# A hybrid attention block and an AdaLN block on one core: ScalarE's steps of attention and planes one slot later, the query norm in the logits, modulation tiles placed anew

## The chip, the cores and the metric

One of the eight cores of a Trainium2 chip runs the whole kernel. The metric is the device time in microseconds of one execution, here the median of three runs. "Slot", "unit" and "tile" below are the kernel's own terms and are explained where it is described.

## The reference, cut to what matters

Sequence 256, width 2048, batch 1, all in fp32. A first block puts 16 meta tokens ahead of the sequence (272 tokens) and runs one layer of two branches. A second block runs on the result with a modulation vector made from a condition `c`.

```python
# first block
q = apply_partial_rope(rms_norm(q_a.reshape(B, T, H_A, HD_A), q_norm_g), *rope_a)   # 8 heads of 128
k = apply_partial_rope(rms_norm(k_a.reshape(B, T, KV_A, HD_A), k_norm_g), *rope_a)
o_a = dsa_attention(q, k, v, qi, ki, wi, chunk_ids, topk)   # indexer scores, top 64 keys, softmax(q.k * d**-0.5)
o_b = hgrn2_chunkwise(qb, 1.0 - f, vb, jnp.log(f))          # gated linear recurrence
merged = sum over the branches of sigmoid(gate) * (y @ w_branch);  x = x + merged @ w_out
# second block
mod = silu(c) @ ada_w + ada_b; sh1, sc1, g1, sh2, sc2, g2 = split(mod, 6)           # ada_w is 2048 x 12288
h  = modulate(rmsnorm(x, norm1_g), sh1, sc1);  hc = modulate(rmsnorm(ctx, norm1_g), csh1, csc1)
q, k, v, f, hy = split(h @ w_in);  kc, vc = split(hc @ w_in[:, 1024:3072])
a = neighbourhood_attention(q, k, v, kc, vc, rpb)
y = merge_groups(a, fourier_mix(f), hyena_mix(hy, ...), mix_norm_g)
x = x + g1 * (y @ w_out)
x = x + g2 * conv_gated_mlp(modulate(rmsnorm(x, norm2_g), sh2, sc2), ...)
return rmsnorm(x, final_norm_g)
```

## The kernel before, in words

**Number format.** Every fp32 value that goes into a large product is split into a high and a low part ("planes", hi and lo) of the type fp32r, and a product is three: hi·hi, lo·hi and hi·lo (lines L1779 to L1781, L1791 to L1793 and L1801 to L1803 for the three layouts). Activations lie with features on partitions (`phi`, `plo`: 16 planes of 128 x 256).

**Slots.** All large products are cut into 668 chunks of 128 x 1024 or equal-sized weights; a unit is four chunks (two in OA and OB). The phases, with their first slot: FB 0, QB 16, IB 32, QI 48, K 64, KA 68, QA 76, VA 92, ZB 100, ZA 116, GA 132, GB 164 (projections of the first block), E 196 (branch products), F 228 (output product, residual), G 260, H 276, IH 292, IF 316, J 324, IQ 340 (projections of the second block: context and stream), OA 372, OB 388 (output), L 404 (MLP up), M0 580 and M1 624 (MLP down). In slot c TensorE multiplies chunk c, ScalarE makes the high part of the weights of chunk c + 4 (`whi`, L558; it waits for TensorE to be done with chunk c), VectorE the low part (`wlo`, L1087; it waits for the high part). There are four buffers of each.

**Side work.** Each engine's order is written out by hand, slot by slot: after the chunk's own step come the steps attached to that slot. They are the recurrence (slots 16 to 91), norms and rotations of attention's chunks from S_NK = 92, the indexer and top k from S_IX = 121, attention from S_AT = 146 (one head and query half per slot, 16 slots), y at S_Y = 167, the squares of the context from S_CQ = 206, the context's planes from S_CX = 231, the stream's planes from S_X1 = 266, filters, Hyena, the Fourier part and neighbourhood attention in the phases G to OA. An instruction that waits holds up all that follows it in its engine's order.

The steps that matter here:
- first planes: ScalarE copies x to `phi` (L862), VectorE makes `plo` (L1109) and the tmp before it (L1112), in slots 4 to 15 and the next.
- norms of the chunks of attention (nine of 13: four of k, the indexer's key, four of q): squares on ScalarE (L767), a mean over the head by a product with a constant matrix (L1931), root on ScalarE (L781), reciprocal and gain on VectorE (L1393, L1394). The rotation is a product with a permutation (L1925) and three VectorE steps (L1401 to L1403).
- attention, head step a: logits on TensorE (L1963), scale, mask and maximum on VectorE (L1444, L1445), exp on ScalarE (L800), division by the sum on VectorE (L1429, L1430), three transposes on TensorE (L1969 to L1971), their copy on ScalarE (L807, L808), three products with v (L1955 to L1957), copy of the result on VectorE (L1438).
- context in F: VectorE multiplies a plane by gain and inverse root (L1512), ScalarE makes `c_hi` (L889), VectorE `c_lo` (L1508) one slot later.
- stream in G and H: VectorE `ptmp` (L1532), ScalarE `stream_hi` (L909), VectorE `stream_lo` (L1537) one slot later.
- neighbourhood attention: the bias is gathered by 16 small loads (L491), two constants by two more (L492, L493); the flip product (L2107) uses them at S_FLIP = 349. L2117 and L982 belong to the mixing of heads behind it.

**Modulation.** `ada_w` is read in 96 tiles of 1 MB. Tiles 0 to 31 are multiplied on TensorE (L1815), 32 to 95 on VectorE in two halves, each in a slot of its own (`ada_half`, L1147 and L1150). At the end of each section of 16 tiles TensorE sums over partitions (L1844); the slots are in `CLOSE`.

**Loads.** SyncE's queue brings everything. Weights (L390) and tiles (L399) share a ring of four raw buffers of 1 MB: entry e is issued when entry e − 4 has been released, by VectorE's `wlo` for weights, by the tile's use for tiles. The order of entries is the order of the units, a tile behind the weights of its unit; where a tile is used is set by `ada_tile_at`.

Of the kernel before, what the change touches and what calls it, by code (L numbers as in the profile page):

```python
# [77 lines left out]
for _n in ("GB", "E"):  # L78
    for _u in range(0, 8, 2):
        ada_tile_at(U0[_n] + _u, -2, 2048)  # L80
for _u in range(8):
    ada_tile_at(U0["F"] + _u, -2, 20480)
for _u in range(8):
    ada_tile_at(U0["G"] + _u, -2, 24320)
for _u in range(7):
    ada_tile_at(U0["IH"] + _u, -2 if _u else 0, 10240)
# [3 lines left out]
for _u, _off in enumerate((2, 1, 0)):  # L90
    ada_tile_at(U0["IQ"] + _u, _off, 8192)
for _u, _off in enumerate((2, 1, 0, -2, -2)):
    ada_tile_at(U0["IQ"] + 3 + _u, _off, (21504, 20480))
for _u in range(0, 12, 2):
    ada_tile_at(U0["OA"] + _u, -2, (21504, 20480))
for _u in range(1, 32, 2):
    ada_tile_at(U0["L"] + _u, -2, 22528)
HOP_F, HOP_IH, HOP_J, FIRST_J, HOP_IQ, HOP_Y = 40, 56, 63, 64, 66, 69


CLOSE = [(0, 15, SH1, ADA_SLOT[15]), (16, 31, SC1, ADA_SLOT[31]), (32, 47, G1, START["F"] + 30), (48, 63, SH2, START["J"] + 8),
         (64, 79, SC2, START["OB"] + 6), (80, 95, G2, ADA_SLOT[95] + 4)]
# [25 lines left out]
TURN_AT.update({(U0["VA"] + 1 + _n // 2, 2 * (_n % 2)): 8 + _n for _n in range(4)})  # L128
# [12 lines left out]
S_BEXP, S_KD, S_KDT, S_OUT = 64, 68, 74, 84  # L141
S_NK, S_IX, S_TOP, S_IX1, S_TOP1, S_AT, S_Y = 92, 121, 129, 133, 141, 146, 167
# [3 lines left out]
S_CQ, S_CX, S_X1, S_SIN = START["E"] + 10, START["F"] + 3, START["G"] + 6, START["G"] + 2  # L146
# [17 lines left out]
def program(nc, A, out):  # L164
# [5 lines left out]
    with ctx:  # L170
# [99 lines left out]
        L, P, PT = R(13920, 2, T), R(14464, 3, T), R(15280, 2, 384)  # L270
# [75 lines left out]
        NNORM = 9  # L346

        def rope_of(c):
# [9 lines left out]
            gain = {1: cols[:, V_KN:V_KN + 1], 2: cols[:, V_QN:V_QN + 1], 3: cols[:, V_IK:V_IK + 1], 0: None}[kind]  # L358
# [6 lines left out]
        def _(sp):  # L365
# [116 lines left out]
            for i in range(8):  # L482
                if i == 3:
# [49 lines left out]
        def _(act):  # L533
# [57 lines left out]
            def evacuate(u):  # L591
# [8 lines left out]
                elif name in ("IB", "VA"):  # L600
                    k = 2 * i + (8 if name == "VA" else 0)
                    act.wait_ge(S("mm"), C0[u + 1])
                    if k >= 1:
                        act.wait_ge(S("vt_tp"), k)
                    for h in range(2):
                        c = nc.scalar.activation(vT[:, h, :], ps[2 * p + h][:, 0:T], ACT.Copy)
# [9 lines left out]
                elif name == "QA":  # L616
                    ev_T(u, q_a[:, 512 * i:512 * i + 512], 256)
# [151 lines left out]
            def attention(s):  # L769
# [23 lines left out]
                a = s - S_AT  # L793
                if 0 <= a < 16:
                    act.wait_ge(S("at_max"), a + 1)
                    if a >= 3:
                        act.wait_ge(S("at_tp"), a - 2)
                    if a >= 2:
                        act.wait_ge(S("at_norm"), a - 1)
                    nc.scalar.activation(P[:, a % 3, :], L[:, a % 2, :], ACT.Exp, bias=small[:, 8 + a % 2:9 + a % 2],  # L800
                                         accum_out=small[:, 10 + a % 2:11 + a % 2]).then_inc(S("at_exp"), 1)
                b = a - 3
# [51 lines left out]
            for c in slots("FB", "GB"):  # L854
# [5 lines left out]
                for kt in PL_AT.get(c, []):  # L860
                    act.wait_ge(S("pl_tmp"), kt + 1)
                    nc.scalar.activation(phi[:, kt, :], xT[:, kt, :], ACT.Copy).then_inc(S("pl_hi"), 1)  # L862
                if (u, q) in TURN_AT:
                    tokens_of(TURN_AT[u, q])
                if u == U0["K"] + 1 and q == 0:
# [6 lines left out]
            def context(s):  # L872
# [8 lines left out]
                if s == S_CQ + 8:  # L881
                    act.wait_ge(S("x_mean"), 2)
# [129 lines left out]
            for c in slots("E", "OB"):  # L1012
# [15 lines left out]
                if 0 <= c - S_X1 < 16:  # L1028
                    kt = c - S_X1
# [34 lines left out]
        def _(dve):  # L1064
# [39 lines left out]
            def first_planes(s):  # L1104


                for kt in PL_AT.get(s - 1, []):
# [17 lines left out]
            def ada_half(c, n, half):  # L1125


                e = ENTRY["ada", n]
# [4 lines left out]
                elif n == HOP_F:  # L1133
                    dve.wait_ge(S("x_mean"), 2)
# [108 lines left out]
            def slot(c):  # L1243
# [20 lines left out]
                if c in ADA_HALF:  # L1264
                    ada_half(c, *ADA_HALF[c])
# [119 lines left out]
            def attention(s):  # L1385
# [40 lines left out]
                b = s - S_AT - 1  # L1426
                if 0 <= b < 16:
                    dve.wait_ge(S("at_exp"), b + 1)
                    chain(v.reciprocal(small[:, 12:13], small[:, 10 + b % 2:11 + b % 2]))  # L1429
                    v.tensor_scalar(P[:, b % 3, :], P[:, b % 3, :], small[:, 12:13], None, ALU.mult).then_inc(S("at_norm"), 1)  # L1430
                    own("at_norm")
                b = s - S_AT - 4
                if 0 <= b < 16:
                    qt, h = b // 8, b % 8
                    dve.wait_ge(S("at_pv"), b + 1)
                    if b < 12:
                        dve.wait_ge(S("at_qk"), b + 5)
                    v.tensor_copy(o_a[:, 256 * h + 128 * qt:256 * h + 128 * qt + 128], ps[4 + b % 2][:, 272:400]).then_inc(S("att_out"), 1)  # L1438
# [901 lines left out]
```

## Time and profile before

| | us |
|---|---|
| median of 3 runs | 2317.23 (2315.51 to 2318.69) |
| the profiled execution | 2316.17 |
| its span | 2314.4 |
| TensorE busy | 2202.2, mean granted clock 0.986 |
| VectorE busy | 1467.1 |
| ScalarE busy | 1029.1 |
| read from memory | 465 MB, 202 GB/s over the span |

The span is from the first to the last instruction that the profiler recorded; the difference of 1.8 us to the time lies around it. In the rows, PE is TensorE, PEld its weight load, DVE VectorE, ACT ScalarE, SP SyncE. A row of the trace gives the start, the time from start to end, the instruction with its output and inputs, how many of them follow each other (x), and in brackets how long the engine had been idle before it and what ended that. An instruction on TensorE is pipelined: the next one begins before the record of the last ends. The granted clock is a share of TensorE's full 2.4 GHz; the lower level is 1.2 GHz.

### The profile page before, as it was taken

The page shows a single profiled execution, that of the slowest core. Times are in us where ns is not written, and L with a number is a line of the kernel's source. Part 1 is how long each engine was busy: PE and PEld are TensorE (multiplying, and loading weights), DVE is VectorE, ACT ScalarE, POOL GpSimd, SP SyncE. Part 2 cuts the span into 40 slices and gives each one's busy share as a digit, 9 for nine tenths or more (in the row PEclk, how much of TensorE's full clock was granted, in tenths as well). Part 3 has the DMA queues.
Part 4 walks back from the last instruction along what each step waited for, and adds up shares of the span by engine and source line. Part 5 has one row for each costly group of instructions (what it writes and reads, how often), then busy time and mean ns, then how long its engine had stood idle before and what let it go on. Part 6 is the DMA issues. An engine that isn't in the chain of part 4 may idle for free.

```text
span 2314.4 us, 37963 instructions
## 1 busy us (share of the span) xinstructions
PE 2202.2 (95%) x16510; PEld 2040.4 (88%) x16510; DVE 1467.1 (63%) x1802; ACT 1029.1 (44%) x1393; POOL 6.2 (0%) x10
## 2 busy tenths in 40 slices
PE   7999999899999997988999799979999999999997
PEld 7889998789899997988788689979999999998885
DVE  6666647757656786767665377776666665555654
ACT  6554334334454553444333354544444443444453
POOL 0000000000000000000000000000000000000000
PEclk9999999999999999999999899989999999999998
DMA  8766565565447876867564655647676766555552
GB/s 295 242 208 193 176 205 182 166 211 164 128 130 253 273 247 200 279 218 252 175 202 154 173 184 184 235 134 264 221 238 219 238 224 205 188 183 198 184 200 91
DMA packets 344260, 469.55 MB, mean 203 GB/s; under 512 B 20445, under 2 KB 318301, under 8 KB 331102
## 3 DMA queue, kind: packets, MB, share of 16 engines
q1 hardware_dynamic: 344094, 467.12, 60.9%
q8 instruction: 130, 2.13, 0.4%
q14 instruction: 36, 0.29, 0.0%
HBM read 465.00 MB, written 2.10 MB: 202 GB/s over the span
## 4 chain that ended last, share of the span: by engine, by line
PE 61%; DVE 6%; ACT 3%; DMA 2%; issue 1%; SPq 1%; DVEq 0%; ACTq 0%
PE ps L1781 14%; PE ps L1779 14%; PE ps L1780 14%; PE ps L1791 3%; PE ps L1793 3%; PE ps L1792 3%; DVE wlo L1087 2%; ACT whi L558 2%; DVE arena L1150 1%; DMA raw<-w_in_dram 1%; SPq L491 1%; PE ps L1802 1%; PE ps L1803 1%; PE ps L1801 1%; PE ps L2142 1%
## 5 line engine op out<-in xcount | busy, mean ns | idle before, releaser
L1087 DVE TENSOR_TENSOR wlo<-raw,whi 128x1024 fp32r<-128x1024 f32 (+1 forms) x668 | 814.3, 1221 | 791.7 <-ACT whi L558 789.7
L558 ACT ACTIVATE whi<-raw 128x1024 fp32r<-128x1024 f32 (+1 forms) x668 | 703.3, 1055 | 1054.5 <-PE ps L1781 836.8
L1779 PE MATMUL ps<-phi,whi 128*128 128x256 f32 (+2 forms) x3744 | 1084.7, 290 | 23.8 <-DVE wlo L1087 15.6
L1780 PE MATMUL ps<-plo,whi 128*128 128x256 f32 (+2 forms) x3744 | 1057.5, 282 | 0.0
L1781 PE MATMUL ps<-phi,wlo 128*128 128x256 f32 (+2 forms) x3744 | 1057.1, 282 | 0.0
L1779 PEld LDWEIGHTS ps<-phi,whi 128*128 128x128 f32 (+1 forms) x3744 | 709.3, 189 | 62.8 <-issue 33.4
L1780 PEld LDWEIGHTS ps<-plo,whi 128*128 128x128 f32 (+1 forms) x3744 | 706.5, 189 | 8.2 <-issue 7.1
L1781 PEld LDWEIGHTS ps<-phi,wlo 128*128 128x128 f32 (+1 forms) x3744 | 709.8, 190 | 0.3
L1150 DVE SCALAR_TENSOR_TENSOR arena<-raw,cst,arena 128x1024 f32<-128x1024 f32 x120 | 153.5, 1280 | 3.4 <-DMA raw<-ada_w_dram 0.3
L1791 PE MATMUL ps<-whi,dhi 128*128 128x512 f32 x352 | 136.9, 389 | 0.0
L1793 PE MATMUL ps<-wlo,dhi 128*128 128x512 f32 x352 | 136.9, 389 | 0.0
L1792 PE MATMUL ps<-whi,dlo 128*128 128x512 f32 x352 | 136.9, 389 | 0.0
L1793 PEld LDWEIGHTS ps<-wlo,dhi 128*128 128x128 f32 x352 | 66.1, 188 | 13.9
L1792 PEld LDWEIGHTS ps<-whi,dlo 128*128 128x128 f32 x352 | 66.1, 188 | 13.7
L1791 PEld LDWEIGHTS ps<-whi,dhi 128*128 128x128 f32 x352 | 66.1, 188 | 13.5
L1779 PE MATMUL ps<-y_hi,whi 128*128 128x256 f32 x256 | 72.1, 282 | 0.0
L1780 PE MATMUL ps<-y_lo,whi 128*128 128x256 f32 x256 | 71.8, 280 | 0.0
L1781 PE MATMUL ps<-y_hi,wlo 128*128 128x256 f32 x256 | 71.6, 280 | 0.0
L1779 PE MATMUL ps<-r_hi,whi 128*128 128x272 f32 x128 | 38.4, 300 | 12.8 <-DVE wlo L1087 12.8
L1780 PEld LDWEIGHTS ps<-y_lo,whi 128*128 128x128 f32 x256 | 48.2, 188 | 0.0
L1781 PEld LDWEIGHTS ps<-y_hi,wlo 128*128 128x128 f32 x256 | 48.2, 188 | 0.0
L1779 PEld LDWEIGHTS ps<-y_hi,whi 128*128 128x128 f32 x256 | 48.0, 187 | 0.0
(340 smaller groups left out, 2347.9 us busy)
## 6 DMA issues: line engine op xcount, KB each, us to landing
raw<-w_in_dram SPq DMA_DIRECT2D x151, 1024.0 KB, 6.1
raw<-ada_w_dram SPq DMA_DIRECT2D x96, 1024.0 KB, 5.0
raw<-ffn_w_up_dram SPq DMA_DIRECT2D x88, 1024.0 KB, 5.1
raw<-ffn_w_down_dram SPq DMA_DIRECT2D x44, 1024.0 KB, 5.2
raw<-w_out_dram SPq DMA_DIRECT2D x32, 1024.0 KB, 6.1
raw<-w_branch_dram SPq DMA_DIRECT2D x16, 1024.0 KB, 5.6
arena<-xT_dram SPq DMA_DIRECT2D x4, 544.0 KB, 6.5
arena<-ctxT_dram SPq DMA_DIRECT2D x1, 2048.0 KB, 10.0
```

Of the source, the lines that this page charges most:

```text
L491: sp.dma_start(Uraw[64 * rq:64 * rq + 64, 6 * h:6 * h + 6, :], src).then_inc(S("rpb_in"), 16)
L558: nc.scalar.activation(whi[c % 4][:, 0:w], src, ACT.Copy).then_inc(S("split_hi"), 1)
L1087: v.tensor_tensor(wlo[c % 4][:, 0:w], src, whi[c % 4][:, 0:w].bitcast(F32), ALU.subtract).then_inc(S("split_lo"), 1)
L1150: t = v.scalar_tensor_tensor(total, x, by, R(ADA_SUM[n - 1][half], 1024), ALU.mult, ALU.add)
L1779: mm(o, wh[:, k], xk, start=st, stop=False)
L1780: mm(o, wh[:, k], yk, start=False, stop=False)
L1781: l = mm(o, wl[:, k], xk, start=False, stop=en)
L1791: mm(o, xk, wh[:, k], start=st, stop=False)
L1792: mm(o, yk, wh[:, k], start=False, stop=False)
L1793: l = mm(o, xk, wl[:, k], start=False, stop=en)
L1801: mm(o, xh[:, kt, tt], wh[:, k], start=kt == 0, stop=False)
L1802: mm(o, xl[:, kt, tt], wh[:, k], start=False, stop=False)
```

## The change

- **First planes.** ScalarE's copy comes one slot after tmp, VectorE's `plo` two (before: the same slot and one).
- **Query norm.** The four chunks of q leave the list of norms (`NNORM` 9 to 5). When QA is evacuated, ScalarE squares each half into `sqq` and copies it with the gain. In slot 94 (`S_QN`) TensorE makes 16 products of one column, whose results are the means of squares of each head and query half; ScalarE takes the root in slot 95, VectorE the reciprocal times `scale` in slot 98. The logits are multiplied by that column in place of `scale`. The turning of v into tokens comes one slot later.
- **Attention.** exp, division, transposes, copies, products with v and the copy of their result come one slot later against the logits. P has four buffers, not three, and some regions lie elsewhere.
- **Context.** The 16 tmp steps go from slots 231 to 246 to slots 216 to 231 (`S_CT`).
- **Stream.** `stream_hi` one slot, `stream_lo` one slot later against `ptmp`.
- **Modulation tiles.** A tile's half is now VectorE's last work of its slot. Tiles 32 to 43 are used in slots 162, 166, 170, 178, 182, 186, 194, 198, 202, 210, 214, 218; 44 to 47 in 226, 234, 242, 250; 48 to 55 as before; 56 to 60 in 294 to 310, every fourth; 61 to 65 in 314, 318, 322, 330, 334; 66 to 72 in 342 to 366, 73 to 79 in 370 to 394, every fourth; 80 to 95 as before. Before: 32 to 39 in 162 to 218, every eighth, 40 to 47 in F's units, every fourth from 226 to 254; 66 to 73 in 342, 345, 348, 354, 357, 360, 362, 366. Two closes move by four slots.
- **Small loads.** The 18 loads for neighbourhood attention are issued before unit IQ2 in place of IQ3.

```diff
 for _n in ("GB", "E"):
-    for _u in range(0, 8, 2):
+    for _u in (0, 1, 2, 4, 5, 6):
         ada_tile_at(U0[_n] + _u, -2, 2048)
-for _u in range(8):
+for _u in range(0, 8, 2):
     ada_tile_at(U0["F"] + _u, -2, 20480)
-for _u in range(7):
-    ada_tile_at(U0["IH"] + _u, -2 if _u else 0, 10240)
+for _u in range(1, 8):
+    ada_tile_at(U0["IH"] + _u, -2, 10240)
-for _u, _off in enumerate((2, 1, 0)):
-    ada_tile_at(U0["IQ"] + _u, _off, 8192)
-for _u, _off in enumerate((2, 1, 0, -2, -2)):
-    ada_tile_at(U0["IQ"] + 3 + _u, _off, (21504, 20480))
-for _u in range(0, 12, 2):
+for _u in (1, 2, 3):
+    ada_tile_at(U0["IQ"] + _u, -2, 8192)
+for _u in (4, 5, 6, 7):
+    ada_tile_at(U0["IQ"] + _u, -2, (21504, 20480))
+for _u in range(0, 14, 2):
     ada_tile_at(U0["OA"] + _u, -2, (21504, 20480))
...
-        NNORM = 9
+        NNORM = 5
...
-                if i == 3:
+                if i == 2:
                     sp.wait_ge(S("y2_set"), 2)
                     sp.wait_ge(S("ada_tp"), 4)
...
                 elif name == "QA":
-                    ev_T(u, q_a[:, 512 * i:512 * i + 512], 256)
+                    act.wait_ge(S("mm"), C0[u + 1])
+                    if i == 0:
+                        act.wait_ge(S("lv_sel"), 32)
+                    if i == 3:
+                        act.wait_ge(S("kd_mm"), 8)
+                    for h in range(2):
+                        nc.scalar.activation(sqq[i][:, 256 * h:256 * h + 256], ps[2 * p + h][:, 0:256], ACT.Square).then_inc(S("x_sq"), 1)
+                        c = nc.scalar.activation(q_a[:, 512 * i + 256 * h:512 * i + 256 * h + 256], ps[2 * p + h][:, 0:256], ACT.Copy,
+                                                 scale=cols[:, V_QN:V_QN + 1])
...
-                a = s - S_AT
+                a = s - S_AT - 1
                 if 0 <= a < 16:
                     act.wait_ge(S("at_max"), a + 1)
...
-                b = a - 3
+                b = s - S_AT - 4
...
-                for kt in PL_AT.get(c, []):
+                for kt in PL_AT.get(c - 1, []):
...
+                if c == S_QN + 1:
+                    act.wait_ge(S("x_mean"), 2)
+                    nc.scalar.activation(rq, ps[6][:, 0:16], ACT.Sqrt, bias=epsc).then_inc(S("x_root"), 1)
...
-                if 0 <= c - S_X1 < 16:
-                    kt = c - S_X1
+                if 0 <= c - S_X1 - 1 < 16:
+                    kt = c - S_X1 - 1
                     stream_hi(0, kt, modL[:, kt:kt + 1])
...
-                for kt in PL_AT.get(s - 1, []):
+                for kt in PL_AT.get(s - 2, []):
...
-                if c in ADA_HALF:
-                    ada_half(c, *ADA_HALF[c])
...
+                if s == S_NK + 6:
+                    dve.wait_ge(S("x_root"), 2)
+                    chain(v.reciprocal(rqs, rq))
+                    v.tensor_scalar(rqs, rqs, scale, None, ALU.mult).then_inc(S("sel"), 1)
...
-                    chain(v.scalar_tensor_tensor(L[:, a % 2, :], ps[4 + a % 2][:, 0:T], scale, selb[:, a // 8, :], ALU.mult, ALU.add))
+                    chain(v.scalar_tensor_tensor(L[:, a % 2, :], ps[4 + a % 2][:, 0:T], rqs[:, 2 * (a % 8) + a // 8:2 * (a % 8) + a // 8 + 1], selb[:, a // 8, :], ALU.mult, ALU.add))
...
                 attention(c)
+                ada_half(c)
...
-                kt = s - S_CX
+                kt = s - S_CT
                 if 0 <= kt < 16:
                     v.scalar_tensor_tensor(ctxT[:, kt, :], ctxT[:, kt, :], gains[:, 16 + kt:17 + kt], invc, ALU.mult, ALU.mult).then_inc(S("pl_tmp"), 1)
...
-                if 1 <= kt < 17:
-                    stream_lo(0, kt - 1, modL[:, kt - 1:kt])
+                if 2 <= kt < 18:
+                    stream_lo(0, kt - 2, modL[:, kt - 2:kt - 1])
...
+                if c == S_QN:
+                    pe.wait_ge(S("x_sq"), 4 + 8)
+                    pe.wait_ge(S("hg_root"), 4)
+                    for j in range(16):
+                        l = mm(ps[6][:, j:j + 1], sqq[j // 4][:, 128 * (j % 4):128 * (j % 4) + 128], mean1[:, 0:1], start=True, stop=True)
+                    l.then_inc(S("x_mean"), 1)
...
-                b = a - 3
+                b = a - 4
                 if 0 <= b < 16:
                     pe.wait_ge(S("at_norm"), b + 1)
```

## Rows read from the trace of the kernel before

**Rows 1.** The page: busy time of the engines, and GB/s in 40 slices.

```profile
PE 2202.2 (95%) x16510; PEld 2040.4 (88%) x16510; DVE 1467.1 (63%) x1802; ACT 1029.1 (44%) x1393; POOL 6.2 (0%) x10
GB/s 295 242 208 193 176 205 182 166 211 164 128 130 253 273 247 200 279 218 252 175 202 154 173 184 184 235 134 264 221 238 219 238 224 205 188 183 198 184 200 91
```

**Rows 2.** Windows: start:end, us, busy of PE, PEld, DVE, ACT, POOL, PEclk, DMA share, GB/s.

```profile
400.30:474.30 74.00, 65.49 (x452) 53.95 (x455) 50.80 (x50) 25.49 (x38) 0.00 (x0) 0.95 0.52 171
594.30:666.80 72.50, 66.02 (x484) 59.50 (x482) 39.79 (x87) 30.16 (x76) 0.00 (x0) 0.98 0.34 107
761.50:853.00 91.50, 91.50 (x771) 91.45 (x771) 72.35 (x89) 54.31 (x57) 0.00 (x0) 1.00 0.79 265
853.00:965.60 112.60, 97.17 (x779) 93.47 (x778) 81.77 (x107) 44.83 (x57) 0.00 (x0) 0.98 0.72 235
965.60:1076.50 110.90, 99.76 (x781) 96.97 (x780) 77.34 (x97) 47.80 (x68) 0.00 (x0) 0.97 0.71 238
1276.80:1427.90 151.10, 135.94 (x1010) 126.54 (x1009) 85.88 (x123) 62.74 (x107) 0.00 (x0) 0.94 0.57 179
```

**Rows 3.** Waits: engine, line, what it waited for: us in total, times, longest.

```profile
ACT phi L909 <- DVE ptmp L1532: 51.6, 31, 3.4
ACT c_hi L889 <- DVE arena L1512: 45.4, 16, 3.9
ACT arena L800 <- DVE small L1445: 41.7, 16, 2.9
```

**Rows 4.** Timeline of one slot of F, by engine: start, us, instruction, idle before.

```profile
902.93 1.28 DVE L1150 SCALAR_TENSOR_TENSOR arena<-raw,cst,arena 128x1024 f32<-128x1024 f32 x1
...
904.52 0.48 DVE L1512 SCALAR_TENSOR_TENSOR arena<-arena,gains 128x256 f32<-128x256 f32 x1
906.52 1.23 DVE L1087 TENSOR_TENSOR wlo<-raw,whi 128x1024 fp32r<-128x1024 f32 x1 [1.52 <-ACT whi L558]
...
905.04 0.51 ACT L889 ACTIVATE c_hi<-arena,modC 128x256 fp32r<-128x256 f32 x1 [3.94 <-DVE arena L1512]
...
907.80 0.39 PE L1779 MATMUL ps<-phi,whi 128*128 128x256 f32 x1 [2.29 <-DVE wlo L1087]
```

**Rows 5.** Timeline of IQ: SyncE's loads, and TensorE's two stalls.

```profile
1299.57 0.99 SPq L390 DMA_DIRECT2D raw<-w_in_dram  x2
...
1301.86 15.99 SPq L491 DMA_DIRECT2D arena<-na_rpb_dram  x16
...
1325.09 1.22 PE L2107 MATMUL ps<-arena 128*128 128x512 f32 x1 [12.05 <-DMA arena<-k_flip_dram]
...
1360.55 0.69 PE L2117 MATMUL ps<-ident,arena 128*128 128x128 f32 x2 [3.12 <-ACT ptmp L982]
```

**Rows 6.** Timeline of TensorE in attention: the longest stall.

```profile
601.69 0.45 PE L1955 MATMUL ps<-arena 16*128 16x128 f32 x2 [3.76 <-ACT arena L808]
```

**Rows 7.** Timeline of TensorE: products of the norms, rotations, and small products.

```profile
421.88 1.02 PE L1931 MATMUL ps<-arena,mean 128*128 128x512 f32 x2
422.33 0.68 PE L1779 MATMUL ps<-phi,whi 128*128 128x256 f32 x1
...
452.19 1.15 PE L1925 MATMUL ps<-arena 128*128 128x512 f32 x1 [2.47 <-DVE arena L1403]
...
470.37 1.12 PE L1925 MATMUL ps<-arena 128*128 128x512 f32 x2 [1.50 <-DVE arena L1403]
...
269.98 1.16 PE L1873 MATMUL ps<-arena 128*128 128x128 f32 x8
...
274.09 0.29 PE L1992 MATMUL ps<-ident,arena 16*128 16x16 f32 x2
```

**Rows 8.** The stage QB: a window, as in rows 2, and the longest stall.

```profile
67.10:101.70 34.60, 29.71 (x243) 26.45 (x243) 23.54 (x38) 20.17 (x23) 5.30 (x3) 1.00 0.77 248
...
85.07 1.06 PE L1815 MATMUL ps<-raw,cst 128*32 128x512 f32 x8 [2.31 <-DMA raw<-ada_w_dram]
```

**Rows 9.** The page's DMA issues: what, KB each, us from issue to landing.

```profile
arena<-ctxT_dram SPq DMA_DIRECT2D x1, 2048.0 KB, 10.0
```

## What I expect, and why

> **What bounds the kernel now.** I read the page's first parts first: TensorE is busy for 2202.2 of 2314.4 us, VectorE for 63% of them, ScalarE for 44% [rows 1]. So only time in which TensorE stands still, runs at its lower clock, or does work that can be dropped can be gained: 112 us idle, and with the mean granted clock of 0.986 at most 0.014 × 2314 = 32 us of clock.
>
> Then the windows, one per stage [rows 2]. The reader is to see a stage that is full (761.5 to 853, stage E: 32 slots in 91.5 us, 2.86 a slot, TensorE busy all of it at clock 1.00) beside stages with the same 768 main products that take longer: F with 112.6 us and 779 records, G and H with 110.9 and 781. The stage of query norms (400.3 to 474.3) has 8.5 us idle at clock 0.95, attention (from 594.3) 6.5 at 0.98, IQ with what follows 15.2 at 0.94.
>
> Then what ScalarE waits for [rows 3]: in F 45.4, in G/H 51.6 and in attention 41.7 us for VectorE, at 16 to 31 steps. Idle time of ScalarE costs nothing by itself; here it does, since the weight split stands behind that wait in ScalarE's order, and VectorE waits for the split. A slot of F shows the loop [rows 4]: after half a modulation tile at 902.93, VectorE makes tmp at 904.52; ScalarE starts c_hi at 905.04 after 3.94 us of idleness, then the split (1.05); VectorE starts wlo at 906.52 after 1.52 idle; TensorE wants it at 907.80 and has stood for 2.29. The loop is tmp 0.4 + c_hi 0.4 + split 1.05 + wlo 1.2 + c_lo 0.4 = 3.45 us, and 1.2 more in the slots that hold half a tile. TensorE wants 2.86.
>
> **The change part by part.** All is set against the profiled execution: 2316.17 us, 1.8 of it outside the span; it stands 1.1 below the median, 2317.23.
>
> *F.* The context's 16 tmp steps go to slots 216 to 231, and eight tile units become four in F and two more in each of GB and E. c_hi then waits for something that was ready slots before: the loop is cut. What stays is E's pace plus 1.0 for 8 further narrow records: 112.6 − 91.5 − 1.0 = **−20.1**.
>
> *G and H.* stream_hi comes one slot after tmp, stream_lo two after, which cuts the same loop. VectorE's own work in a unit of 4 slots is then 4 × 1.2 (wlo) + 2 × 1.2 (tile) + 4 × 0.85 (lo and tmp) = 10.6 us against TensorE's 11.5, so it keeps up narrowly. E's pace plus 3.0 for 10 further records, some of them wide: 110.9 − 91.5 − 3.0 = **−16.4**. What it costs if that cover is gone is rival A.
>
> *IQ.* The stall is 12.05 us at 1325.09, for the DMA of the flip matrix, and 3.12 at 1360.55, for ScalarE behind it [rows 5]. SyncE issued weights at 1299.57 and only then the 18 small loads, which took its queue from 1301.86 on for 16 us and more. They stand one unit earlier after the change, the tiles there go two slots before a unit's end, and what held the ring until 1299.57 (tile 66, used in slots 342 and 343) goes with it. I put their issue near 1276 and the last landing near 1300; TensorE's slot 349 is at 1313. Moved past on SyncE: the second half of IQ2's weights, then 17 us later, but no longer behind tile 66. Idle −15.2; the clock at 0.94 over 151.1 us costs 9.1, of which I take 8.5, what follows the stalls: **−23.7**.
>
> *Attention.* exp, norm, transposes and PT copy come one slot later, with four buffers of P. Before, ScalarE ran the PT copy behind an exp that waited for VectorE's maximum of the same slot, and TensorE stood 3.76 us for that copy at 601.69 [rows 6]. After, exp's maximum is a slot old. Idle 6.5 and clock 0.02 × 72.5 = 1.5: **−8.0**, at worst −5, if 0.2 us stays in each of 16 slots. The slot more at its end is free: y is made 5 slots behind it.
>
> *Query norm.* Removed on TensorE: 4 mean products 512 wide. The product behind one starts at 422.33 and lasts 0.68, not the usual 0.29, so TensorE was taken from 421.88 to 422.72 [rows 7]: 4 × 0.84 = −3.4. The stall before the chunks' rotation is up to 2.47 us (452.19) for a normalized chunk and 1.50 for one without norm (470.37); of 8.5 us idle I take 3.0, and of 0.05 × 74 = 3.7 us of clock 3.4. Added: 16 products of one column, which no row shows. Bounds are 0.15 each (two 16-column transposes take 0.29 at 274.09) and 0.29 (four 128-column products in eight records take 1.16 at 269.98), that is 2.4 to 4.6 for 16; I take 3.2, nearer the first, as one column is nearer to 16. Nothing hides them. Sum 3.4 + 3.0 + 3.4 − 3.2: **−6.6** (−8 to −4).
> Added waits: these products wait in slot 94, with the chunk stream behind them, for Squares of slot 91 and a recurrence step about as old. ScalarE's evacuation of VA waits for the products; behind it stand splits that TensorE wants 4 slots later. 8 Squares of about 0.3 us (a plane of this width takes 0.51 with its overlap, rows 4) lie in ScalarE's 56% of free time. I cost these at nothing, and at one slot, 2.9 us, if the cover is gone.
> On the price of a short product the Trainium skill ("TensorE: Matmul & The Clock Gate", "LDWEIGHTS (loading the stationary operand)") says that a weight load takes its number of columns divided by 1.2, in ns, whatever the contraction: 107 ns for 128. With two records to a product as in the rows, 16 of them would come to an estimated 3.4 us. No row here shows such a product.
>
> *First planes in QB.* 4.9 us idle in that stage, the longest piece 2.31 for a tile that arrives late [rows 8], come from ScalarE and VectorE passing planes to and fro, which frees ring entries late too. With one and two slots between: **−4.6**, at least −2.5, as a load is what ends most of it.
>
> Sum: 20.1 + 16.4 + 23.7 + 8.0 + 6.6 + 4.6 = 79.4, and 2316.2 − 79.4 = 2236.8. I hold back 3.2, since stages that ran late gave the DMAs and VectorE time that they no longer have: **2240**.
>
> **The rivals.** (A) *Loads or VectorE become the bound of E to H.* For: E now also carries tmp (16 × 0.4) and two more tiles (4 halves of 1.2), and the context's 2 MB queue behind a tile, 10.0 us to land by themselves [rows 9]; E already moves 265 GB/s at a share of 0.79; G and H want 3 MB per unit, 273 GB/s at 11.5 us; VectorE is at 92% there. Against: E has no idleness, and slices of the page reach 295 and 279 GB/s [rows 1]. Price: 8 units of G/H late by 1 to 2.5 us each, 8 to 20: 2248 to 2260, 2252 the likeliest. 25%.
> (B) *The change doesn't do what it says in G/H*: the loop stays, by a wait that the diff leaves (sums of a section, filters): 2240 + 16.4 = 2256. 10%.
> (C) *IQ's stall stays.* The 18 loads wait first for semaphores of the stage before; if these come late, SyncE stands there with weights behind it: 2240 + 23.7 = 2264. Against: it was the ring that came last at 1299.57. 8%.
> (D) *Slower than before*, by the clock. TensorE's waits change place, and with them where it is granted 1.2 GHz. To eat 79 us, 160 us of full-speed work in E to H and IQ would have to run at that level, and from there on it is 2316 and more; before, 2 × 32 = 64 us at most were, and the stretches are in stages with gaps (E, without them, is at 1.00). 2%.
> The same page of the Trainium skill ("What's actually happening") has the throttled level as the one TensorE is at without activity; the rows agree, and by it D is the less likely.
>
> **How the numbers follow.** Forecast 55%, A 25%, B 10%, C 8%, D 2%. Low end: 2236.8, less 1.4 (norm at its good bound), less 7, half of the 32 us of clock that the terms above leave (32 − 19): 2228. High end: C's 2264 with 2 us of spread holds A to C singly. About 0.2% is what a measurement of this kernel can tell from no change; all cases but D lie below 2312: faster 96%, the same 2%, slower 2%, D's chance and as much for a mishap between.
>
> **What would show it.** Right: F and G/H at 91 to 96 us each at clock 1.00; ScalarE's waits on the three steps of rows 3 under 5 us each; small loads issued about as TensorE reaches slot 336, and nothing idle before the flip product; no wait for the PT copy. Wrong: TensorE waiting for splits that wait for loads, over 8 us in E to H (A); ScalarE still behind VectorE there (B); one-column products of over 0.3 us; digits of the clock below 9 in E to H (D).

## The result, and the profile after

The changed kernel takes 2242.54 us (median of 4 runs, 2241.26 to 2243.54) against 2316.55 before on the same chip: a ratio of 0.9682, with a 95% interval of 0.967 to 0.9695. The forecast was 2240.0, with 2228 to 2266 as its range. The profiled execution of the changed kernel took 2243.54 with a span of 2241.7, so the span fell by 72.7 us. The sum of the prediction's terms said 79.4, and the forecast, with 3.2 held back, 76.2.

The page of the changed kernel, busy time of the engines, granted clock and GB/s in 40 slices:

```profile
PE 2186.1 (98%) x16534; PEld 2034.5 (91%) x16534; DVE 1453.4 (65%) x1796; ACT 1028.9 (46%) x1394; POOL 6.2 (0%) x10
...
PEclk9999999999999999999999999989999999999998
...
GB/s 318 248 197 192 190 190 172 205 194 176 145 150 256 314 232 266 252 279 221 181 206 155 239 165 206 244 166 233 223 237 233 228 233 188 182 190 199 189 191 92
```

TensorE is busy for 98% of the span, not 95 [rows 1]; the time that it stands still fell from 112.2 to 55.6 us, its busy time by 16.1. Of these 16.1 at most 10.5 are clock: 34.4 us of work ran at the half level before, 13.4 after. The windows of the changed kernel (columns as in [rows 2]) stand for the first 34.6 us of QB, VA, ZB, GA, F, G with H, and IQ:

```profile
67.40:102.00 34.60, 34.60 (x289) 31.82 (x289) 23.35 (x36) 19.46 (x20) 5.31 (x3) 1.00 0.76 252
365.50:401.40 35.90, 35.58 (x262) 32.52 (x265) 24.16 (x25) 14.04 (x26) 0.00 (x0) 0.95 0.62 203
401.40:465.90 64.50, 58.82 (x447) 50.62 (x448) 35.33 (x45) 21.17 (x32) 0.00 (x0) 1.00 0.60 196
526.80:648.50 121.70, 121.70 (x944) 112.09 (x943) 84.18 (x167) 58.53 (x123) 0.00 (x0) 1.00 0.46 142
836.10:929.70 93.60, 92.77 (x783) 91.59 (x782) 68.00 (x89) 45.10 (x57) 0.00 (x0) 1.00 0.73 239
929.70:1023.90 94.20, 94.16 (x776) 92.99 (x776) 77.27 (x97) 48.85 (x68) 0.00 (x0) 1.00 0.88 291
1222.60:1355.10 132.50, 131.97 (x1010) 123.68 (x1009) 84.08 (x121) 63.12 (x107) 0.00 (x0) 1.00 0.63 196
```

Against [rows 2]: F from 112.6 to 93.6, G and H from 110.9 to 94.2, IQ from 151.1 to 132.5, all at clock 1.00 and with 0.8 us of idleness or less. The stage of the norms (ZB) went from 74.0 to 64.5, but VA ahead of it grew from 31.0 to 35.8. Of the three waits in [rows 3], those of the context's c_hi and of attention's exp are gone from the list of waits. The one for ptmp still stands there:

```profile
ACT phi L926 <- DVE ptmp L1556: 11.7, 19, 2.3
```

Most of that isn't in G and H. The same line makes the planes of the MLP at the start of L, and there it waits 8.3 us, 15 times, before the change as after it. In G and H it waited 43.3 us of the 51.6, and now waits 3.4. The list of waits for that window alone, of the kernel before and of the changed one:

```profile
ACT phi L909 <- DVE ptmp L1532: 43.3, 16, 3.4
ACT phi L926 <- DVE ptmp L1556: 3.4, 4, 1.7
```

By stage, the ends of the slots read from the trace of either kernel (us):

| stage | before | after | change | forecast |
|---|---|---|---|---|
| QB | 55.6 | 50.1 | −5.5 | −4.6 |
| IB | 68.0 | 69.6 | +1.5 | 0 |
| VA and ZB (query norm) | 105.1 | 100.4 | −4.7 | −6.6 |
| GA and GB (attention) | 226.3 | 217.8 | −8.5 | −8.0 |
| F | 112.6 | 93.6 | −19.0 | −20.1 |
| G and H | 110.9 | 94.2 | −16.7 | −16.4 |
| IH | 98.9 | 97.3 | −1.6 | 0 |
| IQ | 151.1 | 132.6 | −18.5 | −23.7 |

FB is 0.2 longer, and the others are within 0.1. IB's 1.5 us isn't shown to be of the change: TensorE runs there at half clock for 3.41 us from 130.5 on. Such a stretch (in one case of twice the length) is in seven of the thirteen profiled executions of the changed kernel and of the variants that follow; in the other six, with the same instructions there, IB takes 68.0 as before. IH's 1.6, for which no term stood, is nearly all in slot 298, 5.98 us before and 4.55 after: a wait of 1.16 us for a step of VectorE is gone.

### The profile page after: what moved, and what is told of

It reads as the page before. It is cut to its first block, busy times and chain, and to the rows that moved or that the text cites. A ratio compares the mean times of both kernels' runs of the same rounds, so it can differ in the third digit from the quotient of the medians.

```text
span 2241.7 us, 37995 instructions
## 1 busy us (share of the span) xinstructions
PE 2186.1 (98%) x16534; PEld 2034.5 (91%) x16534; DVE 1453.4 (65%) x1796; ACT 1028.9 (46%) x1394; POOL 6.2 (0%) x10
## 4 chain that ended last, share of the span: by engine, by line
PE 94%; DVE 3%; ACT 2%; DMA 1%; issue 0%; SPq 0%; DVEq 0%; ACTq 0%
PE ps L1805 23%; PE ps L1807 22%; PE ps L1806 22%; PE ps L1819 4%; PE ps L1817 4%; PE ps L1818 4%; PE ps L1899 1%; PE ps L1828 1%; PE ps L1829 1%; PE ps L1827 1%; PE ps L1841 1%; ACT whi L561 1%; DVE wlo L1104 1%; PE ps L2176 1%; PE ps L2109 1%; PE ps L2103 1%
## 6 DMA issues: line engine op xcount, KB each, us to landing
arena<-ctxT_dram SPq DMA_DIRECT2D x1, 2048.0 KB, 10.5
```

## The experiments

Each kernel is the changed one with the edit shown. Their medians compare with 2242.5 us. Where a difference is only some 2 us, it is the stage in the trace that says how much of it is the edit's.

### What cut the loop: the shift of ScalarE's step, or the tile's place

The prediction gave F's whole gain to the tmp steps' new place and G's and H's to the shift. But the diff moves three things in the same stages: the distance of ScalarE's step from tmp, the place of a tile's half in VectorE's slot, and the slots of the tiles. The first run undoes the shift in G and H:

```diff
-                if 0 <= c - S_X1 - 1 < 16:
-                    kt = c - S_X1 - 1
+                if 0 <= c - S_X1 < 16:
+                    kt = c - S_X1
...
-                if 2 <= kt < 18:
-                    stream_lo(0, kt - 2, modL[:, kt - 2:kt - 1])
+                if 1 <= kt < 17:
+                    stream_lo(0, kt - 1, modL[:, kt - 1:kt])
```

> The changed kernel with one thing undone: stream_hi in tmp's own slot and stream_lo one slot behind, as before; the tiles' halves stay at the end of VectorE's slot. Theory 1 (the prediction's: the shift alone cuts the loop in G and H): G and H go from 94 us back to about 110 together, total 2257 to 2259. Theory 2 (a tile's half at the end of the slot had already taken 1.2 us out of the loop, since VectorE works on it while ScalarE makes hi and the split): the loop is 3.45 us in every one of the 16 slots against TensorE's 2.88, so 16 x 0.57 less the lead that the planes start with, 3 to 9 us: 2246 to 2251.

Measured 2251.53 us (2250.69 to 2251.81), ratio to before 0.9722 (0.9707 to 0.9736): 9.0 more than the changed kernel, not 15 to 17, and half a microsecond above the upper end of theory 2. One of H's slots in that run, timeline by engine:

```profile
988.92 0.48 DVE L1561 SCALAR_TENSOR_TENSOR plo<-ptmp,modL,phi 128x256 fp32r<-128x256 f32 x1
989.44 0.48 DVE L1556 SCALAR_TENSOR_TENSOR ptmp<-arena,gains 128x256 f32<-128x256 f32 x1
989.84 1.28 DVE L1170 SCALAR_TENSOR_TENSOR arena<-raw,cst,arena 128x1024 f32<-128x1024 f32 x1
991.45 1.23 DVE L1104 TENSOR_TENSOR wlo<-raw,whi 128x1024 fp32r<-128x1024 f32 x1 [0.33 <-ACT whi L561]
...
989.96 0.51 ACT L926 ACTIVATE phi<-ptmp,modL 128x256 fp32r<-128x256 f32 x1 [1.67 <-DVE ptmp L1556]
990.38 1.04 ACT L561 ACTIVATE whi<-raw 128x1024 fp32r<-128x1024 f32 x1
...
989.07 0.39 PE L1827 MATMUL ps<-whi,c_hi 128*128 128x256 f32 x1 [0.54 <-DVE wlo L1104]
992.73 0.39 PE L1827 MATMUL ps<-whi,c_hi 128*128 128x256 f32 x1 [0.53 <-DVE wlo L1104]
```

The reader is to see the tile's half at 989.84 run while ScalarE does hi and the split: VectorE is idle for only 0.33 us before wlo, where it was idle for 1.52 in F's slot before [rows 4]. The loop is 992.73 − 989.07 = 3.66 us whether a half is in the slot or not; TensorE would take 2.88, so each slot is 0.8 longer, of which 0.54 stands in the brackets as idleness. G doesn't become longer at all, 48.0 us where it has 48.1 with the shift; H has it all, 54.3 for 46.1. By the trace the low parts are ready 6.4 us ahead of TensorE when the loop begins in G, and that lead is used up, at the end by 0.8 us a slot, before TensorE feels anything.

The second undoes only the half's place:

```diff
+                ada_half(c)
                 k = CLOSE_AT.get(c - 2)
...
                 attention(c)
-                ada_half(c)
```

> The changed kernel with one thing undone: a tile's half stands right behind wlo in VectorE's slot, as before, not at its end. Theory 1 (the shift alone is what counts): within 1.5 us of the changed kernel in every stage, 2242 to 2244. Theory 2 (the half ahead of tmp and lo still delays them): with the shift there is a whole slot of room, so it too expects under 2 us. Rival: E and F, where y's and the context's steps stand behind the half, become late and cost 5 us or more: 2248 and up.

Measured 2242.52 us (2241.69 to 2244.14), every stage as in the changed kernel within 0.6 (IH, where a part of its 1.6 comes back). Alone, the place is worth nothing.

The third and fourth are the same question in F:

```diff
-S_CQ, S_CT, S_CX, S_X1, S_SIN = START["E"] + 10, START["E"] + 20, START["F"] + 3, ...
+S_CQ, S_CT, S_CX, S_X1, S_SIN = START["E"] + 10, START["F"] + 3, START["F"] + 3, ...
```

> The changed kernel with one thing undone: the 16 tmp steps of the context are back in slots 231 to 246, in the same slots as ScalarE's c_hi; four tiles in F stay. Theory 1 (tmp's place is the whole of F's gain): F goes from 93.6 us back to about 112, total 2260. Theory 2 (tiles and their place in the slot were a good part): the loop is 3.45 us in 16 slots against 2.86, F +6 to +10, total 2249 to 2253, and E gains nothing since it has no idleness.

Measured 2251.77 us (2250.91 to 2252.82); F 102.9 us, 9.3 more than 93.6, all the rest unchanged.

```diff
-    for _u in (0, 1, 2, 4, 5, 6):
+    for _u in range(0, 8, 2):
         ada_tile_at(U0[_n] + _u, -2, 2048)
-for _u in range(0, 8, 2):
+for _u in range(8):
     ada_tile_at(U0["F"] + _u, -2, 20480)
```

> The changed kernel with one thing undone: eight tiles in F's units and four each in GB's and E's, as before; tmp stays in E's last slots. Theory (with tmp out of F, VectorE's own work of a unit is 4 x 1.2 + 2 x 1.2 + 4 x 0.4 + the residual, about 10 us against TensorE's 11.5): F within 2 us of 93.6, total 2242 to 2245. Rival (F's loads or VectorE could not carry eight tiles): F +5 to +10, with splits waiting for DMA: 2248 to 2253.

Measured 2242.45 us (2241.4 to 2243.49); F 93.1 us. Four tiles fewer in F bring nothing once tmp is out of it.

Edits that are each worth 0 or 9 us alone can be worth 16 or more together. The fifth run makes three of these edits at once, the shift's, tmp's place and the half's place:

> The changed kernel with three things undone together: stream_hi and stream_lo in their old slots, the context's tmp steps back in F, and a tile's half right behind wlo (in F four tiles, not eight). Theory (the half's place counts only while the loop through hi, the split and wlo stands, and then adds its whole 1.2 us): G and H come back to about 110 us (before: 110.9), that is 7 us more than without the shift alone; F, with 8 halves in 16 slots' worth of tmp steps (before 16), to 102.9 + 5 = 107 to 110; total 2268 to 2274. Rival (parts add up, and the half's place is worth nothing as it was alone): G and H 102.3, F 102.9, total 2260 to 2262.

Measured 2273.95 us (2272.62 to 2275.21), ratio 0.9819 (0.9805 to 0.9834). Its windows, F and then G with H:

```profile
836.00:943.70 107.70, 97.24 (x783) 93.83 (x782) 72.35 (x100) 44.93 (x58) 0.00 (x0) 0.98 0.64 208
943.70:1054.30 110.60, 100.06 (x776) 96.53 (x775) 77.25 (x97) 47.70 (x68) 0.00 (x0) 0.97 0.71 236
```

G and H are back at 110.6, where they were 110.9 [rows 2]: 8.1 us come with the shift undone, 8.4 more with the half's place, which by itself was worth 0. VectorE's rows in the loop of that run:

```profile
1018.43 1.23 DVE L1104 TENSOR_TENSOR wlo<-raw,whi 128x1024 fp32r<-128x1024 f32 x1 [1.53 <-ACT whi L561]
1019.57 1.28 DVE L1170 SCALAR_TENSOR_TENSOR arena<-raw,cst,arena 128x1024 f32<-128x1024 f32 x1
1020.77 0.48 DVE L1561 SCALAR_TENSOR_TENSOR plo<-ptmp,modL,phi 128x256 fp32r<-128x256 f32 x1
1021.28 0.48 DVE L1556 SCALAR_TENSOR_TENSOR ptmp<-arena,gains 128x256 f32<-128x256 f32 x1
1023.29 1.23 DVE L1104 TENSOR_TENSOR wlo<-raw,whi 128x1024 fp32r<-128x1024 f32 x1 [1.52 <-ACT whi L561]
```

From wlo to wlo it is 4.86 us with a half in it, and 3.67 without. The clock has no share in the 8.4 us, though two stretches of 3.41 us at half clock lie in G and H here: four slots with two halves take 17.05 us, with such a stretch in them, and 14.67 with the halves' place alone put right, and the difference is the two halves. TensorE was slower in one slot and waited less in the next. F is at 107.7, 9.3 and 4.7 more; the last 4.9 to 112.6 belong to the other four tiles, by exclusion. So the half's place counts only while the loop stands: it shortens a slot with a half from 4.86 to 3.66 us. The shift cuts the loop, and then the place is worth nothing.

### IQ: the small loads' place, or the tiles'

```diff
-                if i == 2:
+                if i == 3:
                     sp.wait_ge(S("y2_set"), 2)
```

> The changed kernel with one thing undone: the 18 small loads of neighbourhood attention are issued before unit IQ3 rather than IQ2; the tiles' new places in IQ stay. Theory 1 (what SyncE's queue waited for was the ring held by tile 66, and the issue one unit earlier is what cures it): issued from some 1245 to 1257, the flip matrix landed near 1263, TensorE wants it near 1258: 4 to 6 us of idleness and 2 of clock, total 2247 to 2251. Theory 2 (the tiles' places alone were enough): no stall, 2242 to 2244. A return of the whole 18.5 us (2261) would say that the tiles' places do nothing.

Measured 2247.99 us (2245.23 to 2248.92); IQ 139.7 us, 7.2 more. TensorE's stall in that run:

```profile
1261.78 2.08 PE L2141 MATMUL ps<-arena 128*128 128x512 f32 x2 [5.16 <-DMA arena<-k_flip_dram]
```

The other run puts the tiles back where they were:

```diff
-for _u in (1, 2, 3):
-    ada_tile_at(U0["IQ"] + _u, -2, 8192)
-for _u in (4, 5, 6, 7):
-    ada_tile_at(U0["IQ"] + _u, -2, (21504, 20480))
-for _u in range(0, 14, 2):
+for _u, _off in enumerate((2, 1, 0)):
+    ada_tile_at(U0["IQ"] + _u, _off, 8192)
+for _u, _off in enumerate((2, 1, 0, -2, -2)):
+    ada_tile_at(U0["IQ"] + 3 + _u, _off, (21504, 20480))
+for _u in range(0, 12, 2):
     ada_tile_at(U0["OA"] + _u, -2, (21504, 20480))
```

> The changed kernel with one thing undone: tiles 66 to 73 in IQ in their old slots (342, 345, 348, 354, 357, 360, 362, 366) and 74 to 79 in OA and OB; the small loads before IQ2 stay. Theory 1 (the place of the small loads is enough): they are issued before the ring is held by tile 66, no stall at the flip product, IQ within 2 us of 132.6, total 2242 to 2245. Theory 2 (the ring held by tile 66 delays the weights of IQ2 so that splits come late too): IQ +5 to +12, total 2247 to 2254.

Measured 2251.25 us (2250.74 to 2251.6); IQ 141.9, 9.4 more. SyncE issues the small loads as early as in the changed kernel (1223.34, there 1221.91) and the flip product doesn't wait for them, but a later product, of the mixing of heads, waits for ScalarE:

```profile
1223.34 11.73 SPq L494 DMA_DIRECT2D arena<-na_rpb_dram  x16
...
1294.12 1.11 PE L2151 MATMUL ps<-ident,arena 128*128 128x128 f32 x4 [4.63 <-ACT ptmp L999]
```

and in its list of waits:

```profile
ACT whi L561 <- DMA raw<-w_in_dram: 37.6, 9, 7.9
```

With old places, a tile that is used late in its unit holds its ring entry, and weights are issued late: the next ones behind the small loads at 1243.92, in the changed kernel at 1233.77. ScalarE stands 37.6 us in splits that wait for loads (6.0 in the changed kernel), and its ptmp behind a split comes late for TensorE. Two slots ahead of that one are 0.8 and 2.0 us longer because wlo is late. Both edits were needed: undone alone they cost 7.2 and 9.4. These two don't share out the 18.5 that the stage gained, since they weren't undone together.

### The query norm: what the one-column products cost

Each of the 16 products leaves two records in the trace (x32 below). The run doubles them:

```diff
-                    for j in range(16):
+                    for j in list(range(16)) + list(range(16)):
                         l = mm(ps[6][:, j:j + 1], sqq[j // 4][:, 128 * (j % 4):128 * (j % 4) + 128], mean1[:, 0:1], start=True, stop=True)
```

> The changed kernel with the 16 one-column products of the query norm made twice into the same columns (32 products). In the changed kernel the trace shows 3.63 us for them, and behind them a stretch of 3.4 us at half clock without any idleness before it. Theory 1 (a product costs its two weight loads, 2 x 0.11 us): +3.6 us for the products, and the clock falls for as long or for a second stretch, +0 to +2: 2246 to 2248.5. Theory 2 (most of the 3.63 us is waiting at the start, and 16 more cost 16 x 0.15 = 2.4): 2244.5 to 2245.5.

Measured 2248.25 us (2247.83 to 2248.58), 5.7 more; VA 42.6 us for 35.8, 6.8 more, while IB's stretch, 1.5 us, isn't in this execution. The products in the changed kernel's timeline:

```profile
376.07 3.63 PE L2027 MATMUL ps<-mean,arena 128*128 128x1 f32 x32
```

with windows over them and over what follows:

```profile
376.07:379.50 3.43, 3.43 (x34) 3.43 (x32) 1.23 (x1) 1.06 (x1) 0.00 (x0) 1.00 1.02 311
379.70:383.10 3.40, 3.40 (x12) 2.93 (x13) 0.92 (x1) 0.49 (x1) 0.00 (x0) 0.50 0.26 88
```

The same two views of the run with 32 products:

```profile
374.12 9.92 PE L2027 MATMUL ps<-mean,arena 128*128 128x1 f32 x64
```

```profile
378.20:388.40 10.20, 10.20 (x44) 9.73 (x45) 1.78 (x1) 0.49 (x1) 0.00 (x0) 0.50 0.02 8
```

At the full clock a record is 0.11 us, 3.5 us for 16 products, and the weight load is busy all of it. At 379.7, with no idleness before it, the clock goes to its half level for 3.4 us, 1.7 us of loss. In the doubled burst it falls after 4.1 us, while the products still run, and stays for 10.2; from there on a record takes 0.21. So the price of the change here is 5.2 us, not 3.2: the slot with the products takes 9.11 us, 3.94 before.

The remedy tried is two lots of eight:

```diff
-                if c == S_QN:
-                    pe.wait_ge(S("x_sq"), 4 + 8)
-                    pe.wait_ge(S("hg_root"), 4)
-                    for j in range(16):
+                if c in (S_QN, S_QN + 1):
+                    if c == S_QN:
+                        pe.wait_ge(S("x_sq"), 4 + 8)
+                        pe.wait_ge(S("hg_root"), 4)
+                    for j in range(8 * (c - S_QN), 8 * (c - S_QN) + 8):
...
-                if c == S_QN + 1:
+                if c == S_QN + 2:
                     act.wait_ge(S("x_mean"), 2)
```

> The changed kernel with its 16 one-column products of the query norm in two lots of eight, behind the chunks of slots 94 and 95, and ScalarE's root one slot later. In the changed kernel 16 in a row take 3.63 us and a stretch of 3.41 us at half clock follows with no idleness before it; doubled to 32, the half-clock stretch grew to 10.24 us. Theory 1 (an unbroken burst of such products is what lowers the clock): no half-clock stretch near slot 95, VA 1.7 us shorter, total 2240 to 2241.3. Theory 2 (their number in the neighbourhood counts, not the burst): the stretch stays, within 0.5 us of the changed kernel, 2242 to 2243.

Measured 2239.66 us (2239.56 to 2241.59), ratio 0.9676 (0.9663 to 0.969). VA is 34.2 us, 1.6 less, and at clock 1.00; the two lots in the timeline, and VA's window:

```profile
374.05 1.84 PE L2026 MATMUL ps<-mean,arena 128*128 128x1 f32 x16
...
380.86 1.95 PE L2026 MATMUL ps<-mean,arena 128*128 128x1 f32 x16
```

```profile
363.50:397.70 34.20, 33.88 (x261) 31.13 (x264) 24.07 (x25) 14.13 (x25) 0.00 (x0) 1.00 0.64 212
```

The intervals of this ratio and of the changed kernel's overlap, so the gain stands on the stage, 1.6 us, not on the medians; of their difference of 2.9, 1.5 is IB's stretch, which this execution doesn't have. The rule isn't without exception: of ten profiled executions with 16 in a row nine have the stretch, one (the run on attention, below) has not and shows VA at 34.2 too; of two with lots of eight, none has it. With one exception in ten, two executions are thin ground for the lots being the cure.

### Attention and first planes, undone alone

Steps of attention one slot earlier again, on all three engines, with four buffers kept:

```diff
-                a = s - S_AT - 1
+                a = s - S_AT
...
-                b = s - S_AT - 4
+                b = s - S_AT - 3
...
-                b = a - 5
+                b = a - 4
```

> The changed kernel with one thing undone: exp, division, transposes, their copy, products with v and the result's copy one slot earlier, as before; four buffers of P and the query norm in the logits stay. Theory (the copy stands behind an exp that waits for the maximum of its own slot): GA from 121.7 us back to about 131, GB from 96.0 to 94.7, total 2250 to 2252, with a wait of some 3 to 4 us for the copy once. Rival (part of the gain came from the half tiles' place or the buffers): GA under 127, total under 2247.

Measured 2251.48 us (2251.31 to 2251.7): GA 132.3, GB 94.7, so 9.2 more. (GA lost 9.9 us by the change and GB gained 1.4, as the last steps moved into it.) The copy is late again, in the timeline and in the list of waits:

```profile
592.38 0.45 PE L1981 MATMUL ps<-arena 16*128 16x128 f32 x2 [3.99 <-ACT arena L822]
```

```profile
ACT arena L814 <- DVE small L1468: 42.7, 16, 3.0
```

Before, it was 3.76 and 41.7 us [rows 3, 6].

The steps of the first planes as before:

```diff
-                for kt in PL_AT.get(c - 1, []):
+                for kt in PL_AT.get(c, []):
...
-                for kt in PL_AT.get(s - 2, []):
+                for kt in PL_AT.get(s - 1, []):
```

> The changed kernel with one thing undone: ScalarE's copy of the first planes in tmp's own slot and VectorE's low part one slot behind, as before. Theory (passing the planes to and fro delays splits and the tiles' ring entries): QB from 50.1 us back to 55.6, total 2247 to 2248.5. Rival (the loads end most of that idleness and come late anyway): QB 51 to 53, total 2243.5 to 2245.5.

Measured 2246.96 us (2245.58 to 2248.48); QB 53.8 us, 3.7 more, between what the theory and the rival said. Its stalls are 0.49 and 0.84 us for tiles' loads where before had 0.90 and 2.31; the ones for planes and wlo are the same. The change has nothing else in these slots, so the 1.8 us that the undoing doesn't bring back may be the loads' own spread from run to run; that was not tested.

### A version that is faster than both

What is left in the norms' stage are waits of 1.50 and 0.33 us before the rotations, the first as in [rows 7]. VectorE's rotation of a chunk stands behind a wlo that waits for its slot's split. In the last kernel it stands ahead, in a function of its own that is called before slot(c), together with the two lots:

```diff
             for c in slots("FB", "GB"):
+                rotate(c)
                 slot(c)
...
-                c -= 1
-                if 0 <= c < 13 and odd:
-                    chunk, w, sh, (cs, sn), gain, _ = rope_of(c)
-                    dve.wait_ge(S("nk_rot"), c + 1)
...
```

> As the run with two lots of eight, and VectorE's three rotation steps of a chunk stand ahead of wlo in their slot, not behind it. In the changed kernel TensorE stands 1.50 or 0.33 us before each rotation product of slots 100 to 118, since VectorE's previous rotation waits in its order behind a wlo that waits for the split of that slot: 5.7 us in ZB and 1.8 in ZA. Theory (only the order on VectorE makes this wait): ZB 64.5 to 59 or 60, ZA 60.9 to 59 or 60, total 2233 to 2236. Rival (the rotation then waits for TensorE's product, and wlo behind it comes late and holds the chunks): gain under 2 us, 2239 to 2242, with waits of chunks for wlo in its place.

Measured 2231.24 us (2229.78 to 2231.57), ratio 0.9635 (0.9622 to 0.9648), against 0.9682 (0.967 to 0.9695) for the changed kernel: 11 us less, 8 of them beyond the run with the two lots alone. ZB and ZA:

```profile
399.10:456.40 57.30, 57.30 (x448) 50.28 (x451) 37.14 (x49) 21.19 (x32) 0.00 (x0) 1.00 0.67 221
456.40:514.90 58.50, 58.50 (x459) 50.10 (x459) 33.75 (x50) 24.32 (x41) 0.00 (x0) 1.00 0.66 213
```

64.5 and 60.9 became 57.3 and 58.5, 9.6 less where the idleness was 7.5, and more than the 6 or 7 expected; nothing waits for wlo there. That the other 2.1 are gaps too short for the idle column is a guess.

## Why the prediction was right, and where it was not

**The bound.** Right: 56.6 us of the 72.7 came as idleness of TensorE and up to 10.5 as its clock. The rest lies in its busy time, in part in gaps too short for the idle column; no work of ScalarE or VectorE had to become less for it.

**F and G/H.** −19.0 and −16.7 for −20.1 and −16.4. The mechanism is shown by the runs that undo it; that 4.9 us of F's belong to tiles rests on exclusion. Rows 3 were misread in G/H (43.3 of the 51.6 us are there), without effect on the sum, which was taken from the windows. What the prediction had wrong is the share: it gave all of F's to tmp's new place and all of G's and H's to the shift. The loop with a half inside (4.65 us in its own sum, 4.86 measured) and the loop without (3.45, and 3.66 measured) are both slower than 2.86, and the new place in the slot alone takes the first to the second. It named the two lengths and didn't ask what the half's move, which the diff also had, would do to them. It also left out the lead of 6 us. VectorE kept up as narrowly as it said: in 958 to 1004 it is busy for 43.5 of 46.0 us, and TensorE for all of it. F's other 1.1 us: 0.8 is idleness.

**IQ.** −18.5 for −23.7, the largest miss, and one of counting. Idle −14.6 came, for 15.2. The clock's 8.5 did not: it was read off as the mean clock times the window, but most of the half-clock stretch lay over the stall itself. Windows of the kernel before, the stall and what follows it, then the second stall's end:

```profile
1313.00:1325.10 12.10, 0.05 (x2) 0.01 (x1) 0.00 (x0) 0.00 (x0) 0.00 (x0) 0.62 0.82 180
1325.10:1329.50 4.40, 4.40 (x14) 3.37 (x15) 0.41 (x1) 1.50 (x2) 0.00 (x0) 0.51 1.09 388
1360.50:1363.60 3.10, 3.05 (x10) 2.69 (x11) 2.90 (x6) 3.02 (x6) 0.00 (x0) 0.50 0.98 385
```

The half clock costs nothing while the engine is idle. Only 4.4 us of the first stretch, of 13.65, and 3.0 of the second, of 3.41 from 1360.2 on, lay over work: (4.4 + 3.0) / 2 = 3.7, and 14.6 + 3.7 = 18.3 of the 18.5. Of the cause it had half. The prediction held tile 66's ring entry responsible for the late small loads, and that has a part: with new tiles and the loads in their old place the stall is 5.16 us, not 12.05. But issued one unit earlier they are on time with old tiles too, and 9.4 us are lost all the same, through splits that wait for weights; that path it didn't have. It put the issue near 1276, where TensorE begins IQ, slot 340 [rows 2]. That is where it came (1221.91, with slot 340 from 1222.58 on); the 336 among its signs doesn't agree with its own figure.

**Query norm.** −4.7 for −6.6. The removed work was right: ZB lost 9.5 us for 9.8 (idle 8.5 to 5.7, forecast 5.5; clock 0.95 to 1.00). The one-column products were mis-sized: 3.5 us for 3.2, within the bounds, plus 1.7 us of clock that no term had. The rule of the Trainium skill ("TensorE: Matmul & The Clock Gate", "LDWEIGHTS (loading the stationary operand)"), by which the prediction had 3.4 us in a sentence of its own, agrees with the trace at the full clock: 0.11 us a record for 128 columns. At the half level a record took 0.21 us in the doubled run, which the rule doesn't say.

**Attention.** −8.5 for −8.0; the steady 0.2 us a slot went too (slots of 4.9 to 5.0 us became 4.68).

**First planes.** −5.5 for −4.6; the run that undoes them gives 3.7 of it.

**What was held back.** 3.2 us for loads and VectorE. Not needed: G and H ran at 291 GB/s and a share of 0.88 without idleness, and E kept its 91.6 us. Rival A didn't happen at all, B, C and D neither. That the forecast of 2240 lies so near 2242.5 is in part luck: the hold-back was for loads and VectorE, and it covered a part of the clock counted too high. IH's unforeseen 1.6 and IB's 1.5 cancelled.

Not run: the query norm undone alone, so that its −4.7 rests on the two stages' times and the runs on its products; F's loop with eight tiles and the half at the end of the slot; the two edits in IQ undone together; and more tiles in E than the change has.

## What to carry to other kernels

A step that two engines pass to and fro within one slot makes a loop: add up its parts, with all that stands between them in either engine's order, and compare with the slot of the engine that should set the pace. One slot's distance cuts it, and what else stood in the loop then costs nothing; so undo edits together as well as alone before sharing the gain out. Count a lower clock only over work that sets the pace, never over idleness. Look at what a burst of tiny products does to it. And before a wait is put to a stage, ask for it in that stage's window: one line of the kernel can serve two.

## What the runs showed of the hardware

A run of 16 fp32 products with one moving column (32 records) took 3.43 us, all of it weight loads, at 0.11 us a record. In nine of ten executions TensorE's clock went from 2.4 to 1.2 GHz for 3.4 us, 0.0 to 1.1 us behind the last of them, with no idleness before it. With 32 in a row it fell after 4.1 us and stayed there for 10.2, and a record took 0.21. In two lots of 1.8 us it didn't fall in either of two. The Trainium skill ("TensorE: Matmul & The Clock Gate", "What's actually happening") ties the level to how busy TensorE has been; in these rows its record was busy without a gap and the clock fell. Why it did, and what sets the one exception apart, is open.

In G and H 291 GB/s over 94 us, at a DMA share of 0.88, left TensorE with 0.04 us of idleness; one split there waited 2.8 us for a load, and that didn't reach TensorE.
